# A gate vector's row made by two 512-column products and a trip over DRAM, split products reordered, a centring step moved up

## The reference, cut to what matters

```
mod    = split(silu(c) @ ada_w + ada_b, 6)           # six vectors of 1024
a      = rmsnorm(x, g_pre) * (1 + mod[1]) + mod[0]
b_gate, c_gate, v = split(a @ sc_w_in, 3)
y      = (b_gate * conv3(c_gate * v, sc_conv)) @ sc_w_out
x      = x + mod[2] * rmsnorm(y, g_post)
f      = square(relu((rmsnorm(x, g_pre_ff) * (1 + mod[4]) + mod[3]) @ mlp_w_in)) @ mlp_w_out
x      = x + mod[5] * rmsnorm(f, g_post_ff)
```

## Time and profile before

| | |
|---|---|
| time, median of 3 runs | 748.65 us (748.03 to 748.76) |
| the profiled execution's own time | 748.62 us |
| its span in the trace | 746.9 us (1.7 us lie around it) |
| PE busy | 739.9 us, 99% of the span |
| DVE busy | 551.4 us, 74% |
| ACT busy | 366.4 us, 49% |
| POOL busy | 12.1 us, 2% |
| PE clock granted | full in all 40 slices |

### The profile page before, as it was taken

The page is one execution under the profiler, slowest core; times in us unless marked ns, Lnnn a source line. Parts: engine busy times, 40 slices in busy tenths (PEclk is TensorE's granted clock), DMA queues, the critical chain, the costliest instruction groups (busy, mean ns, idle before and its releaser), DMA issues.

```text
span 746.9 us, 13280 instructions
## 1 busy us (share of the span) xinstructions
PE 739.9 (99%) x5368; PEld 690.4 (92%) x5368; DVE 551.4 (74%) x767; ACT 366.4 (49%) x455; POOL 12.1 (2%) x29
## 2 busy tenths in 40 slices
PE   8999999999999999999999999999999999999998
PEld 8889956999998888899979999999999999999998
DVE  4669888865556734499899967859889988887441
ACT  4145233745553333496555356585566655554330
POOL 0000000000000000020000011000000000000000
PEclk9999999999999999999999999999999999999999
DMA  9999998364566968436545242437554555443640
GB/s 306 349 366 375 380 360 299 129 211 169 177 208 208 346 187 252 169 128 226 173 166 179 111 162 99 133 128 261 184 211 149 197 198 190 151 149 121 205 138 29
DMA packets 53712, 152.71 MB, mean 204 GB/s; under 512 B 3040, under 2 KB 34144, under 8 KB 43424
## 3 DMA queue, kind: packets, MB, share of 16 engines
q1 hardware_dynamic: 52832, 149.43, 58.4%
q0 software_dynamic: 544, 1.84, 0.7%
q10 hardware_dynamic: 288, 0.76, 0.3%
HBM read 150.97 MB, written 1.05 MB: 204 GB/s over the span
## 4 chain that ended last, share of the span: by engine, by line
PE 85%; DVE 8%; ACT 2%; SPq 2%; issue 1%; DMA 1%; DVEq 0%; ACTq 0%
PE ps L1534 19%; PE ps L1533 19%; PE ps L1535 19%; PE ps L1715 4%; PE ps L1713 4%; PE ps L1714 4%; PE ps L1760 4%; PE ps L1617 3%; DVE w_lo L934 3%; DVE cacc L1307 2%; DMA raw<-in_ada 1%; SPq L420 1%; ACT w_hi L561 1%; PE ps L1884 1%; PE ps L1883 1%
## 5 line engine op out<-in xcount | busy, mean ns | idle before, releaser
L934 DVE TENSOR_TENSOR w_lo<-raw,w_hi 128x2048 fp32r<-128x2048 f32 (+2 forms) x116 | 246.0, 2123 | 83.1 <-ACT w_hi L561 83.1
L1533 PE MATMUL ps<-a_hi,w_hi 128*128 128x256 f32 x1024 | 289.9, 283 | 0.0
L1535 PE MATMUL ps<-a_hi,w_lo 128*128 128x256 f32 x1024 | 289.5, 283 | 0.0
L1534 PE MATMUL ps<-a_lo,w_hi 128*128 128x256 f32 x1024 | 289.4, 283 | 0.0
L561 ACT ACTIVATE w_hi<-raw 128x2048 fp32r<-128x2048 f32 (+2 forms) x116 | 205.6, 1777 | 98.9 <-PE ps L1715 43.4
L1533 PEld LDWEIGHTS ps<-a_hi,w_hi 128*128 128x128 f32 x1024 | 193.9, 189 | 1.2 <-issue 0.6
L1534 PEld LDWEIGHTS ps<-a_lo,w_hi 128*128 128x128 f32 x1024 | 192.5, 188 | 0.6 <-issue 0.5
L1535 PEld LDWEIGHTS ps<-a_hi,w_lo 128*128 128x128 f32 x1024 | 192.4, 188 | 0.0
L1534 PE MATMUL ps<-up_lo,w_hi 128*128 128x256 f32 x192 | 54.4, 283 | 0.0
L1535 PE MATMUL ps<-up_hi,w_lo 128*128 128x256 f32 x192 | 54.3, 283 | 0.0
L1533 PE MATMUL ps<-up_hi,w_hi 128*128 128x256 f32 x192 | 54.2, 283 | 0.0
(11 more groups left out here) (289 smaller groups left out, 949.6 us busy)
## 6 DMA issues: line engine op xcount, KB each, us to landing
raw<-in_w_z_in SPq DMA_DIRECT2D x26, 1024.0 KB, 4.8
raw<-in_w_up SPq DMA_DIRECT2D x22, 1024.0 KB, 4.7
raw<-in_w_mlp_in SPq DMA_DIRECT2D x16, 1024.0 KB, 5.0
raw<-in_w_mlp_out SPq DMA_DIRECT2D x16, 1024.0 KB, 5.9
raw<-in_w_down SPq DMA_DIRECT2D x16, 704.0 KB, 4.1
raw<-in_ada SPq DMA_DIRECT2D x32, 256.0 KB, 7.4
raw<-in_ada_half SPq DMA_DIRECT2D x8, 1024.0 KB, 7.3
raw<-in_ada SPq DMA_DIRECT2D x8, 1024.0 KB, 6.4
```

What stands on the lines that cost most here:

```text
L934: e.tensor_tensor(w_lo[:, slot, 0:words], raw[:, unit_slot, 0:words], w_hi[:, slot, 0:words].bitcast(f32), SUB).then_inc(raw_used, 1)
L1533: e.matmul(dst, w_hi[:, slot, cols], hi, start=start, stop=False, skip_group_check=skip)
L1534: e.matmul(dst, w_hi[:, slot, cols], lo, start=False, stop=False, skip_group_check=skip)
L1535: return e.matmul(dst, w_lo[:, slot, cols], hi, start=False, stop=stop, skip_group_check=skip)
```

## The change

It has four parts.

- The order of each split product in tiles k = 6 and 7 becomes high by high, low weight by high activation, high weight by low activation. The first waits for the high parts alone; each low part is waited for by the first product that uses it.
- `mod_sums(2)`, `mods(0, 2)`, the product with the norm's weight, `widen` and `gain_evict` go. In their place PE sums `ada_acc` 0 over partitions straight to rows (`row_sums`, two products of 512 columns with `ones` as weights), in the middle of the second sc_out group. The bias and the norm's weight, which lie as columns, are turned on PE to eight rows of 128 each at k = 1 of the start (`param_columns_turned`), copied by ACT, written by POOL to DRAM (8 KB), and read back by POOL as two rows spread over 128 partitions, 512 KB each, into `y`. DVE adds the one and multiplies by the other (`gain_rows`), ahead of the second mlp_in split.
- The centring of step 22 moves ahead of that step's weight split on DVE.
- The semaphores of part loads 2 to 7 are shared by pairs: one wait for 32 in place of two for 16.

```diff
@@ part loads
-                 .then_inc(part_in[u][piece], 16)
+                 .then_inc(part_in[u if u < 2 else u // 2 + 1][piece], 16)
@@ POOL
-            e.wait_ge(gain_cols, 2)
+            e.wait_ge(rows_copied, 1)
+            e.dma_start(param_rows.rearrange("n (i p) -> i n p", p=P), sc_c[0:DT, 0, :].rearrange("i (n p) -> i n p", n=2))\
+             .then_inc(row_out, 16)
+            e.wait_ge(row_out, 16)
+            e.wait_ge(w_used, USED)
+            e.wait_ge(act_hi, DT)
+            e.wait_ge(act_lo, DT)
+            for n in range(2):
+                e.dma_start(flat(y[:, 4 * n:4 * n + 4, :]), param_rows[n:n + 1, :].broadcast_to([P, D])).then_inc(row_in, 16)
+
+            e.wait_ge(gain_cols, 1)
@@ ACT
+            def param_rows_copied():
+                e.wait_ge(rows_turned, 1)
+                e.activation(sc_c[0:DT, 0, :], ps[0:DT, 6, 0:2 * P], ACT.Copy).then_inc(rows_copied, 1)
...
+                if t == 1:
+                    param_rows_copied()
@@ DVE
-            def gain_evict(dst, n):
+            def gain_rows(dst):
+                e.wait_ge(row_in, 32)
+                start = ch.n
                 for h in range(2):
-                    e.wait_ge(gain_wide, 2 * n + h + 1)
-                    e.tensor_copy(dst[:, h * 512:(h + 1) * 512], ps[:, 6 + h, :]).then_inc(gain_in, 1)
-                e.wait_ge(gain_in, 2 * n + 2)
+                    cols = slice(h * 512, (h + 1) * 512)
+                    e.wait_ge(gain_wide, h + 1)
+                    ch.mark(e.tensor_tensor(dst[:, cols], ps[:, 6 + h, :], flat(y[:, 4 + 2 * h:6 + 2 * h, :]), ADD))
+                for h in range(2):
+                    cols = slice(h * 512, (h + 1) * 512)
+                    ch.wait(start + h + 1)
+                    e.tensor_tensor(dst[:, cols], dst[:, cols], flat(y[:, 2 * h:2 * h + 2, :]), MUL).then_inc(gain_in, 1)
...
             ahead_at(g0)
+            gain_rows(gain_b)
             ahead_at(g0 + 1)
-            mods(0, 2)
-            e.tensor_tensor(gain_post[:, :], mod[:, 16:24], pcol("gains", 8, 8), MUL).then_inc(gain_cols, 1)
             for i in range(2):
                 ada_unit(ring_unit("shift", i), 2 * i, ada_acc[:, 2, :])
-            gain_evict(gain_b, 0)
+            e.wait_ge(gain_in, 2)
@@ PE, split tiles
                     e.matmul(dst, key_split(w_hi, at, at + P), a_hi[:, k, :], start=False, stop=False, skip_group_check=True)
-                    e.matmul(dst, key_split(w_hi, at, at + P), a_lo[:, k, :], start=False, stop=False, skip_group_check=True)
-                    mm = e.matmul(dst, key_split(w_lo, at, at + P), a_hi[:, k, :], start=False, stop=k == DT - 1, skip_group_check=True)
+                    if n == 0 and k == 6 and grp % 2 == 0:
+                        e.wait_ge(key_lo, grp // 2 + 1)
+                    e.matmul(dst, key_split(w_lo, at, at + P), a_hi[:, k, :], start=False, stop=False, skip_group_check=True)
+                    if n == 0 and grp == 0:
+                        e.wait_ge(act_lo, k - 5)
+                    mm = e.matmul(dst, key_split(w_hi, at, at + P), a_lo[:, k, :], start=False, stop=k == DT - 1, skip_group_check=True)
@@ PE, start
+            def param_columns_turned():
+                e.wait_ge(par_in, 16)
+                for n, (name, first) in enumerate((("gains", 8), ("ada_b", 16))):
+                    mm = e.matmul(ps[0:DT, 6, n * P:(n + 1) * P], pcol(name, first, DT), ident[:, :], start=True, stop=True)
+                mm.then_inc(rows_turned, 1)
...
+                if k == 1:
+                    param_columns_turned()
@@ PE, sc_out
+            def row_sums(acc):
+                for h in range(2):
+                    e.matmul(ps[:, 6 + h, :], ones[:, :], acc[:, h * 512:(h + 1) * 512], start=True, stop=True).then_inc(gain_wide, 1)
...
-                        if (c, h) == (1, 0) and k == 4:
-                            widen(gain_post, 0)
+                        if (c, h) == (0, 1) and k == 4:
+                            e.wait_ge(raw_used, ring_unit("half", 7) + 1)
+                            row_sums(ada_acc[:, 0, :])
...
-                    if (c, h) == (0, 1):
-                        e.wait_ge(raw_used, ring_unit("half", 7) + 1)
-                        mod_sums(2, ada_acc[:, 0, :], MISC)
```

More of the change, by code:

```diff
@@ L160, in build_program @@
         gain_pre = sb("gain_pre", [P, DT])
-        gain_post = sb("gain_post", [P, DT])
         gain_pre_ff = sb("gain_pre_ff", [P, DT])
@@ L255, in build_program @@
         x_new = sem("x_new")
-        part_in = [[sem(f"part_in{i}_{h}") for h in range(len(PIECES))] for i in range(PARTS)]
+        part_in = [[sem(f"part_in{i}_{h}") for h in range(len(PIECES))] for i in (0, 1, 2, 4, 6)]
         key_in = [[sem(f"key_in{q}_{h}") for h in range(2)] for q in range(4)]
@@ L275, in build_program @@
         gain_wide = sem("gain_wide")
+        rows_turned = sem("rows_turned")
+        rows_copied = sem("rows_copied")
+        row_out = sem("row_out")
+        row_in = sem("row_in")
+        param_rows = nc.dram_tensor("param_rows", (2, D), f32).ap()
         gain_row_out = sem("gain_row_out")
@@ L689, in sc_copy @@
             def sc_copy(grp):
+                if grp == 0:
+                    e.wait_ge(row_out, 16)
                 if grp < 3:
@@ L980, in pair_sums @@
                 for piece, (i, lo, hi) in enumerate(PIECES):
-                    e.wait_ge(part_in[2 * q][piece], 16)
-                    e.wait_ge(part_in[2 * q + 1][piece], 16)
+                    e.wait_ge(part_in[q + 1][piece], 32)
                     for j in range(lo, hi):
@@ L1080, in token_chain @@
                 behind()
-            MOD_SUMMED, MOD_BANK = (1, 2, 3, 4), (MISC, 0, 1, MISC)
+            MOD_BANK = (0, 1, MISC)
             def mods(number, vector):
-                e.wait_ge(mod_ps, MOD_SUMMED[number])
+                e.wait_ge(mod_ps, number + 1)
                 cols = slice(8 * vector, 8 * vector + 8)
@@ L1229, in scale_columns @@
             def scale_columns():
-                mods(1, 4)
+                mods(0, 4)
                 ch.mark(e.scalar_tensor_tensor(gain_pre_ff[:, :], mod[:, 32:40], 1.0, pcol("gains", 16, 8), ADD, MUL))
-            token_chain("post", 1, gain_b, x_tok, x_t, scale_columns, lambda: mods(2, 3))
+            token_chain("post", 1, gain_b, x_tok, x_t, scale_columns, lambda: mods(1, 3))
             ch.wait()
@@ L1253, in _ @@
                 if j == 7:
-                    mods(3, 5)
+                    mods(2, 5)
                     e.tensor_tensor(gain_post_ff[:, :], mod[:, 40:48], pcol("gains", 24, 8), MUL).then_inc(gain_cols, 1)
@@ L1341, in _ @@
                     scale_first(1)
+                if s == CV_MEAN_STEP:
+                    e.wait_ge(cv_mean, 1)
+                    for i in range(4):
+                        e.scalar_tensor_tensor(cacc[:, i, :], ps[:, STAT, 0:T], -1.0 / SG, cacc[:, i, :], MUL, ADD)\
+                         .then_inc(cv_cent, 1)
                 if s != SG_STEP:
@@ L1396, in _ @@
                     e.tensor_tensor(sq[:, 1, 0:T], cacc[:, 0, :], cacc[:, 1, :], ADD).then_inc(cv_folded, 1)
[L1397 to L1402, removed]
                 if s == CV_VAR_STEP:
@@ L1656, in _ @@
             for k in (6, 7):
-                e.wait_ge(act_lo, k - 5)
+                e.wait_ge(act_hi, k + 1)
                 for grp in range(4):
                     if k == 6 and grp % 2 == 0:
-                        e.wait_ge(key_lo, grp // 2 + 1)
+                        e.wait_ge(key_hi, grp // 2 + 1)
                     mm = by_split_key(k, grp)
@@ L1762, in _ @@
                     mm.then_inc(tok_done, 1)
-                    if (c, h) == (0, 1):
-                        e.wait_ge(raw_used, ring_unit("half", 7) + 1)
-                        mod_sums(2, ada_acc[:, 0, :], MISC)
-            e.wait_ge(mod_read, 1)
             e.wait_ge(gain_in, 2)
```

## The result

| | before | after |
|---|---|---|
| time, median of 5 runs | 748.65 us (748.03 to 748.82) | 744.27 us (744.25 to 744.53) |
| the profiled execution | 748.62 us, span 746.9 | 744.25 us, span 742.3 |

The ratio is 0.9941, 95% interval 0.9930 to 0.9953. In the table of the experiments further down the times are medians of all executions, and the ratios leave out one execution of e1 (1204.42 us at a granted clock of 0.558) and one of e6 (735.91 us at full clock).

What follows compares the result with a forecast made beforehand. The prediction took PE, busy 99% of the span, as the bound. Its terms 1.84 + 0.12 + 0.57 = 2.53 us off 748.62 gave 746.1 us, range 745.5 to 747.6.

Steps and rivals of the forecast that it cites:

- Part 1: Gate vector's row in sc_out: 1.84 us less for PE; POOL's rows over DRAM cost 0, bounds 0 to 1.0 us.
- rivals 1 and 3: At sc_out: POOL's rows delay half units, up to 1.0 us (0.15); DVE becomes the bound, second turn waits 0.6 (0.06).
- Rival 2: POOL's transfers hold up SP's loads by far more than their bytes: 5.0 us at row sums, 751.1; chance 0.05.
- Part 2: Reordered split products at k = 6 and 7, ahead of sc_out: 0.12 us gained, bounds 0 to 0.3.
- Part 3: Centring moved ahead of the split: PE's wait at the squares' sum goes, gain 0.57 us, bounds 0.3 and 0.6.
- Rival 4: Small waits come back: centring and split order give nothing, another releaser being as late; 746.8 us, chance 0.10.
- Part 4: Shared semaphores, four waits become waits on one: nothing taken, bounds 0 and 0.1 us of gain.
- The sum: Whole kernel: 1.84 + 0.12 + 0.57 = 2.53 us off the profiled execution's 748.62, so 746.1 us.

Runs made afterwards that it cites:

- e1: The kernel before with an unused tile of 32 bytes a partition in front of gain_pre_ff; 747.59 us, ratio 0.9987.
- e6: The changed kernel with unused tiles of 96 bytes in front of x and 32 in front of gain_pre_ff; 732.13 us, ratio 0.9755.
- e2: The changed kernel with the unused tile gain_post put back, so all tiles lie where they lay before the change; 746.38 us, ratio 0.9970.
- e10: e2 with POOL's two rows fetched four times over, pair after pair; 751.63 us in one run, 5.3 more than e2.
- e8: The kernel before with only the centring of step 22 moved ahead of that step's weight split; 748.08 us against 748.72, ratio 0.9992.
- e5: The changed kernel with unused tiles of 96 bytes in front of x and of gain_pre_ff; 728.22 us in one execution.
- e12: The kernel before with one unused tile of 96 bytes in front of x and no edit of the change; 732.55 us, ratio 0.9760.
- e9: The changed kernel with unused tiles of 128 bytes in front of x and 96 in front of gain_pre_ff; 739.34 us, ratio 0.9878.

## Why the prediction was right and wrong

**Part 1, right.** Forecast 1.84 us less in sc_out, measured 2.13 - 0.31 = 1.82. The two row products took 1.75 (forecast 1.72). The products at the start cost nothing: PE reached the first pair sum no later than before, whether it waited 0.2 us there, as in after, or 0.9, as in e2. The second half unit took 1.3 us longer to land, as worked out, and DVE started it 0.42 us after it could have; the forecast said 0.5. The loads ahead of it show the price where nothing was taken up: those that SP issued at 60.3, 64.6, 67.9 and 71.3 us took 12.1, 9.8, 8.4 and 7.6 us, against 9.5, 7.0, 5.6 and 5.2 us for the same loads before, 2.4 to 2.8 more each, where the forecast had 2.5 for the two rows. PE waited for none of them. PE's margin at the row sums came out as 0.3 us where I had 0.2, the second `turn` has the 0.67 that the working left it, and rivals 1 and 3 didn't happen. Rival 2 rested on the one slow load, 6.5 us late; no load of SP between 60 and 80 us was later than 2.8, and e10 shows four times the bytes to cost 5.3 us. The transfer of 8 KB took 5.4 us, under half of the 12.0 that I had from its nearest row; nothing waited for it.

**Part 2, right.** Between the first pair sum and sc_out after gains 0.31 - 0.19 and e2 0.18 - 0.06, both 0.12 us, the value taken. The mechanism is the one worked out: the first split product goes ahead, at 51.44, and PE meets DVE's second `key_lo` at the seventh tile's second product, at 54.53. What the kernels are ahead by at the first pair sum (0.19 and 0.06 with the same edits) varies with the transfers at the start; I book it to none of the parts.

**Part 3, right.** Forecast 0.57, measured 0.61 in after; e8, the centring alone, has the squares' sum 0.57 us earlier. Rival 4 fell.

**Part 4.** Nothing forecast, and nothing shows that could be put down to it. It wasn't tested apart.

**The sum, wrong.** For the edits the sum was right: forecast 2.53 us, and by e2 2.6 in the span (746.9 to 744.3), 2.4 in the profiled execution and 2.2 in the medians (748.56 to 746.38 in the same runs). The step that failed is in front of the sum: the working went through instructions, waits and transfers, took each edit's price from those, and let the rest of the kernel stand as it was in the trace, a term put at nothing. I noted that the vector's product goes and never asked what its tile's going moves. That is 746.38 - 744.27 = 2.1 us, nearly half of the gain. No term, no bound and no rival held it, so the range ended at 745.5. (By the upper bounds of parts 2 and 4, which are to set that end, it would be 748.62 - 2.53 - 0.18 - 0.1 = 745.8; the measured time lies below both.) And chance had the sign: had `up_hi` stood 64 bytes lower, the same deletion would have taken the down product from d = 32 to d = 0, by the table 3.3 ns more in each of 528 products, 1.8 us the wrong way. That is an estimate for the down product alone.

## What to carry to other kernels

In a kernel that one engine fills to 99%, the price of its commonest instruction is a term of every forecast: look first whether an edit changes the addresses of what it reads, and multiply. Compare two versions only with the tiles at the same places, by a spacer where one has gone, or a gain of the layout is booked to the edit. And try the layout itself: a single unused tile of 96 bytes a partition was worth 16 us of 748 here, and the whole worked-out change 2.2. The best distance isn't a rule to carry along: it was found by trying, and it differs between the stages of this kernel.

## What the runs showed of the hardware

- PE's distance of starts in float32 products split in three, 256 columns each with a new weight tile, at full clock and with no wait, goes by d: 120.0 ns at d = 0 and 96, 116.7 at 32, 117.8 at 64, 118.7 at 128 and 160, 113.3 or 117.8 at 192, 118.3 at 224. The Trainium skill's page "SBUF — State Buffer", section "Operand start alignment", says where an operand may start, adds that this is about legality and not speed, and that its runs timed nothing. Here 32 bytes are worth 2.2 ns in 120 (from 96 to 64), and 5.0 or 0.5 from 224 to 192.
- The single distances spread too: in the up product of before they lie between 115 and 126 ns, in that of e5 nearly all are 113 or 114.
- In mlp_out the parts are swapped, the weights are streamed, 512 columns each, and the activations `hid` loaded. Its distances move too: 234.3 ns before, 233.3 after and 226.7 in e5. In e5 `hid` lies at d = 0, where the down product is as slow as before, so the values of the 256-column products don't hold for it.
- At d = 192 the same kernel takes one of two levels, by stage and by execution, and its time is spread over 10.9 us in e6 and 10.5 in e12. The engine's granted clock is full in both levels. At that distance the change's own 2.2 us can't be seen: e6 with it has 732.13, e12 without it 732.55.
- Open is what makes it so. PE's weight loads and its streamed reads getting in each other's way would fit a dependence on distance, but no run looks inside. That 256 bytes is the period was assumed and not tried: the tiles of d = 0 and 32 are the ones pushed past the next multiple of 256, and counted modulo 512 they would lie in the other half from all the rest. The values of d = 0, 32, 64, 160 and 224 rest on one kernel each. No distance was tried off the multiples of 32. DVE and ACT write the tiles that were moved, and their accesses were never moved apart from PE's. What picks the level at d = 192 isn't known.
- The lowest times are those with `a_hi` and `a_lo` at d = 192: e6 725.03 to 735.91 us (ratio 0.9755, which leaves open whether it is 2% under the kernel before), e12 725.66 to 736.13, and e5 728.22 in its one execution. Which of them is fastest isn't settled. The fastest with its times within 0.7 us of each other is e9, 739.34 us.
